# Hybrid mixer and experts layer on one core: keys projected first, zeros written by ScalarE, rotations placed ahead of the scores

## The reference

```python
h = rms_norm(x, norm_mix_g[i])
proj = h @ w_in[i]
y_s5 = s5_mixer(proj[..., :r0], ...)        # x[t] = lambda * x[t-1] + B u[t];  y = C x + D u
# RWKV-7: low-rank products of the shifted h
w_log = -softplus(-(w0 + tanh(xw @ w1) @ w2)) - 0.5
a = sigmoid(a0 + (xa @ a1) @ a2)
g = sigmoid(xg @ g1) @ g2
kk = heads(k * k_k);  kk = kk / max(norm(kk), 1e-12)
k = k * (1.0 + (a - 1.0) * k_a)
# per token: state = state * decay + (state . -kk) (kk * a)^T + v k^T;  y = state . r
```

## Time and profile before

| | value |
|---|---|
| median of 3 runs | 1267.28 us (1266.63 to 1267.98) |
| profiled execution | 1267.05 us |
| its span, first to last instruction | 1265.3 us |
| busy: VectorE, ScalarE, GpSimd | 402.3, 205.1, 28.3 us |
| read from memory | 427.89 MB, 339 GB/s over the span |
| mean granted TensorE clock | 0.972 of 2.4 GHz |

### The profile page before, as it was taken

How to read it: one execution, slowest core, us unless ns; L and a number is a source line. 1 busy time by engine, 2 the same in 40 slices (tenths; PEclk the granted TensorE clock), 3 DMA queues, 4 the chain that set the end, 5 groups by cost and what they waited for, 6 DMA issues and landing times. The chain is left out here.

```text
span 1265.3 us, 19269 instructions
## 1 busy us (share of the span) xinstructions
PE 1170.8 (93%) x8190; PEld 514.8 (41%) x8190; DVE 402.3 (32%) x750; ACT 205.1 (16%) x297; POOL 28.3 (2%) x16
## 2 busy tenths in 40 slices
PE   5889688958999999999999999999999999999997
PEld 4678586433333333333333333333333333333333
DVE  8928992572112122122112112211212112211222
ACT  2661012262000010011000001000011000000113
POOL 4100000020000000000000000000000000000000
PEclk8899888979999999999999999999999999999998
DMA  9300207235999999999999999999999999999960
GB/s 326 99 2 3 71 19 292 100 146 223 419 427 426 429 429 428 428 429 428 427 429 430 427 428 430 428 428 429 429 427 429 429 428 427 430 428 427 429 273 33
DMA packets 44237, 429.38 MB, mean 339 GB/s; under 512 B 4817, under 2 KB 15441, under 8 KB 19633
## 3 DMA queue, kind: packets, MB, share of 16 engines
q1 hardware_dynamic: 44016, 428.43, 80.9%
q0 software_dynamic: 192, 0.52, 0.1%
HBM read 427.89 MB, written 1.05 MB: 339 GB/s over the span
## 5 line engine op out<-in xcount | busy, mean ns | idle before, releaser
L1140 PE MATMUL bank<-arena 128*64 128x512 f32 (+5 forms) x5388 | 920.6, 479 | 24.7 <-DMA arena<-in_exp_w_up 19.1
L1140 PEld LDWEIGHTS bank<-arena 128*64 128x64 f32 (+4 forms) x5388 | 316.3, 128 | 605.3 <-issue 541.9
L221 PE MATMUL bank<-arena 64*64 64x64 f32 (+7 forms) x2032 | 175.0, 282 | 27.2 <-DVE arena L603 7.8
L221 PEld LDWEIGHTS bank<-arena 64*64 64x64 f32 (+3 forms) x2032 | 141.6, 160 | 59.8 <-issue 40.8
L1331 ACT ACTIVATE arena<-arena 128x512 f32<-128x512 f32 x32 | 20.1, 629 | 515.4 <-DVE arena L1375 515.4
L1390 DVE COPY arena<-bank 128x512 f32<-128x512 f32 x32 | 22.1, 691 | 234.9 <-PE bank L1140 234.9
L1380 DVE TENSOR_SCALAR arena<-bank 128x512 f32<-128x512 f32 x32 | 22.1, 691 | 211.8 <-PE bank L1140 211.8
L1375 DVE TENSOR_SCALAR arena<-bank 128x512 f32<-128x512 f32 x32 | 22.1, 691 | 188.8 <-PE bank L1140 188.8
L1334 ACT ACTIVATE arena<-bank 128x256 f32<-128x256 f32 x32 | 12.3, 383 | 310.1 <-PE bank L1430 310.1
L1351 DVE TENSOR_TENSOR arena<-bank,par 128x512 f32<-128x512 f32 x33 | 22.8, 692 | 76.4 <-PE bank L1140 76.4
L1331 ACT ACT_TABLE_LOAD x32 | 41.1, 1283 | 1.7 <-PEq L1162 1.2
(11 more groups left out here) (269 smaller groups left out, 459.8 us busy)
## 6 DMA issues: line engine op xcount, KB each, us to landing
arena<-in_exp_w_gate SPq DMA_DIRECT2D x64, 2048.0 KB, 23.4
arena<-in_exp_w_down SPq DMA_DIRECT2D x64, 2048.0 KB, 21.8
arena<-in_exp_w_up SPq DMA_DIRECT2D x64, 2048.0 KB, 25.3
arena<-in_w_in SPq DMA_DIRECT2D x8, 1024.0 KB, 12.1
arena<-in_w_out SPq DMA_DIRECT2D x4, 1024.0 KB, 5.5
arena<-in_ple_w_gate SPq DMA_DIRECT2D x2, 2048.0 KB, 21.7
arena<-in_xT SPq DMA_DIRECT2D x1, 1024.0 KB, 6.1
arena<-in_lora SPq DMA_DIRECT2D x1, 1024.0 KB, 13.6
```

The source lines that it names most:

```text
L221: return nc.tensor.matmul(out, lhsT, rhs, start=start, stop=stop, skip_group_check=True)
L1140: return nc.tensor.matmul(out, lhsT, rhs, start=start, stop=stop, skip_group_check=True)
```

## The change

- `order` becomes k, k, u, u, r, r, v, v. All counts on `proj_done` and `proj_copied` follow it, by `at_place`.
- The zeros are written by ScalarE (`clear`: a copy of one column of `par` with scale 0), in pieces, between its work of the start; those of `taps` come ahead of the tables. GpSimd writes none.
- The sum of squares uses `ones_early`, which VectorE fills, and waits for `eps_ready` instead of the constants' load. ScalarE's squares come behind the state-space exponentials and sines.
- The second low-rank product 1 goes to banks 2 and 3. Product 2 comes behind `project(2)`.
- TensorE: `project(3)`, the sums of the key norms, `project(4)` and `project(5)` come ahead of the taps; `into` follows `stack_u`.
- VectorE: the keys come ahead of the decays, output products and angles behind `k2`, and `phase_off(0)`, `phase_on(0)`, `phase_off(1)` together behind the receptance. `oprod` lies in other units.
- ScalarE's queue follows the others.

```diff
-oprod = [un(a).rearrange("p (n j c) -> p n j c", n=SUB, c=16) for a in (43, 25, 44)]
+oprod = [un(a).rearrange("p (n j c) -> p n j c", n=SUB, c=16) for a in (37, 25, 39)]
...
-root = un(24)[:, 0:T]
+root, ones_early = un(24)[:, 0:T], un(24)[:, 512:512 + P]
...
+LORA_BANK = (5, 2, 5)
...
-order = [0, 1, 4, 5, 2, 3, 6, 7]
+order = [4, 5, 0, 1, 2, 3, 6, 7]
+at_place = [order.index(q) + 1 for q in range(8)]
...
-    nc.gpsimd.memset(un(45), 0.0).then_inc(s["pads_clear"], 1)
-    nc.gpsimd.memset(un(16, 4), 0.0).then_inc(s["pads_clear"], 1)
-    nc.gpsimd.memset(un(20, 4), 0.0).then_inc(s["pads_clear"], 1)
...
-    pool.wait_ge(s["proj_done"], 2)
-    nc.gpsimd.memset(un(2, 2), 0.0).then_inc(s["pads_clear"], 1)
...
-    act.wait_ge(s["xT_in"], 16)
-    for b in range(2):
-        A(sq[:, 4 * b:4 * b + 4, :], xT[:, 4 * b:4 * b + 4, :], ACT.Square).then_inc(s["sq_ready"], 1)
+    def clear(a, n):
+        A(un(a, n), par[:, NPARAM:NPARAM + 1].to_broadcast([P, n * UNIT]), ACT.Copy, scale=0.0).then_inc(s["pads_clear"], 1)
+    act.wait_ge(s["eps_ready"], 1)
+    clear(45, 1)
+    clear(16, 2)
...
+    clear(18, 2)
...
+    act.wait_ge(s["xT_in"], 16)
+    for b in range(2):
+        A(sq[:, 4 * b:4 * b + 4, :], xT[:, 4 * b:4 * b + 4, :], ACT.Square).then_inc(s["sq_ready"], 1)
+    clear(20, 2)
+    clear(22, 2)
...
-    act.wait_ge(s["eps_ready"], 1)
...
-            src = banks[5 + i // 2][:, (i % 2) * T:(i % 2 + 1) * T]
+            src = banks[LORA_BANK[m] + i // 2][:, (i % 2) * T:(i % 2 + 1) * T]
...
-    act.wait_ge(s["pads_clear"], 2)
+    act.wait_ge(s["pads_clear"], 3)
...
-    act.wait_ge(s["pads_clear"], 3)
+    act.wait_ge(s["kk_ready"], 1)
+    A(kksq[:, :, :], kkn[:, :, :], ACT.Square).then_inc(s["kk_squared"], 1)
+    copy_proj(2)
+    lora_out(2)
+    act.wait_ge(s["decay_ready"], 1)
+    A(EL[:, :, :], Lc[:, :, :], ACT.Exp)
+    link(A(chunk_decay[:, :, :], Lc[:, :, CH - 1::CH], ACT.Exp))
+    A(Lc[:, :, :], Lc[:, :, :], ACT.Exp, scale=-1.0)
+    A(lw[:, :, :], lw[:, :, :], ACT.Exp).then_inc(s["exp_ready"], 1)
+    copy_proj(3)
+    act.wait_ge(s["kk_summed"], 1)
+    for b in range(2):
+        m = A(kb[:, 2 * b:2 * b + 2, :], banks[4 + b].rearrange("p (f t) -> p f t", t=T), ACT.Sqrt)
+    m.then_inc(s["kk_root"], 1)
+    act.wait_ge(s["pads_clear"], 5)
...
-    lora_out(2)
+    clear(2, 2)
...
-    copy_proj(2)
-    act.wait_ge(s["pads_clear"], 4)
+    copy_proj(4)
+    copy_proj(5)
+    act.wait_ge(s["pads_clear"], 6)
...
-    act.wait_ge(s["decay_ready"], 1)
...
-    copy_proj(3)
-    act.wait_ge(s["kk_ready"], 1)
-    A(kksq[:, :, :], kkn[:, :, :], ACT.Square).then_inc(s["kk_squared"], 1)
-    copy_proj(4)
-    act.wait_ge(s["kk_summed"], 1)
-    for b in range(2):
-        m = A(kb[:, 2 * b:2 * b + 2, :], banks[4 + b].rearrange("p (f t) -> p f t", t=T), ACT.Sqrt)
-    m.then_inc(s["kk_root"], 1)
-    for n in range(5, 8):
-        copy_proj(n)
+    copy_proj(6)
+    copy_proj(7)
...
+    V.memset(ones_early, 1.0)
...
-    dve.wait_ge(s["g_built"], 2)
-    products(oprod, "o_built", power[:, 0, 1:SUB + 1, :], power[:, 1, 1:SUB + 1, :], cc)
...
-    ts(un(46), un(46), PI, -PI, ALU.min, ALU.max).then_inc(s["table_arg"], 1)
...
+        if H:
+            dve.wait_ge(s["phase_on"], H)
...
-        dve.wait_ge(s["proj_done"], (4, 7)[H])
+        dve.wait_ge(s["proj_done"], (at_place[5], at_place[6])[H])
...
-    dve.wait_ge(s["proj_done"], 1)
-    link(V.memset(EL, 1.0))
-    link(V.memset(EL[:, :, 0::CH], 0.0))
-    dve.wait_ge(s["lora2_copied"], 2)
-    link(ts(lw, lw, -DECAY, None, ALU.mult))
-    link(V.tensor_tensor_scan(un(0), un(1), un(31), 0.0, ALU.mult, ALU.add))
-    tt(lw, Lc, lw, ALU.subtract).then_inc(s["decay_ready"], 1)
-    dve.wait_ge(s["proj_copied"], 4)
+    dve.wait_ge(s["proj_copied"], at_place[5])
...
+    dve.wait_ge(s["lora2_copied"], 2)
+    link(ts(lw, lw, -DECAY, None, ALU.mult))
+    dve.wait_ge(s["proj_done"], at_place[0])
+    link(V.memset(EL, 1.0))
+    link(V.memset(EL[:, :, 0::CH], 0.0))
+    link(V.tensor_tensor_scan(un(0), un(1), un(31), 0.0, ALU.mult, ALU.add))
+    tt(lw, Lc, lw, ALU.subtract).then_inc(s["decay_ready"], 1)
...
-    dve.wait_ge(s["o_padded"], 4)
-    V.memset(mag_run[:, :, 0:1], 0.0).then_inc(s["mag_ready"], 1)
-    phase_off(0)
+    products(oprod, "o_built", power[:, 0, 1:SUB + 1, :], power[:, 1, 1:SUB + 1, :], cc)
...
+    ts(un(46), un(46), PI, -PI, ALU.min, ALU.max).then_inc(s["table_arg"], 1)
...
-    dve.wait_ge(s["proj_done"], 5)
+    dve.wait_ge(s["proj_done"], at_place[2])
...
-    phase_on(0)
-    dve.wait_ge(s["proj_copied"], 6)
+    dve.wait_ge(s["o_padded"], 4)
+    V.memset(mag_run[:, :, 0:1], 0.0).then_inc(s["mag_ready"], 1)
+    dve.wait_ge(s["proj_copied"], at_place[3])
...
+    phase_off(0)
+    phase_on(0)
...
-    pe.wait_ge(s["consts_in"], 16)
+    pe.wait_ge(s["eps_ready"], 1)
...
-        last = mm(banks[7][:, 0:T], ones, sq[:, k, :], k == 0, k == KD - 1)
+        last = mm(banks[7][:, 0:T], ones_early, sq[:, k, :], k == 0, k == KD - 1)
...
+        pe.wait_ge(s["consts_in"], 16)
+        pe.wait_ge(s["lora2_copied"], 4)
...
-    for m in range(3):
+    def lora_second(m):
...
-            if m and i % 2 == 0:
-                pe.wait_ge(s["lora2_copied"], 2 * m - 2 + i // 2 + 1)
-            out = banks[5 + i // 2][:, (i % 2) * T:(i % 2 + 1) * T]
+            if m == 2 and i % 2 == 0:
+                pe.wait_ge(s["lora2_copied"], i // 2 + 1)
+            out = banks[LORA_BANK[m] + i // 2][:, (i % 2) * T:(i % 2 + 1) * T]
...
+    def head_sums(src, bank):
+        for b in range(2):
+            last = mm(banks[bank + b][:, :], head_ones, src[:, 2 * b:2 * b + 2, :], True, True)
+        return last
+    lora_second(0)
+    lora_second(1)
...
+    lora_second(2)
+    project(3)
+    pe.wait_ge(s["consts_in"], 16)
+    pe.wait_ge(s["kk_squared"], 1)
+    pe.wait_ge(s["lora2_copied"], 6)
+    head_sums(kksq, 4).then_inc(s["kk_summed"], 1)
+    project(4)
+    project(5)
...
-    project(3)
...
-    project(4)
-    pe.wait_ge(s["kk_squared"], 1)
-    pe.wait_ge(s["lora2_copied"], 6)
-    for b in range(2):
-        last = mm(banks[4 + b][:, :], head_ones, kksq[:, 2 * b:2 * b + 2, :], True, True)
-    last.then_inc(s["kk_summed"], 1)
-    project(5)
...
```

More of the change, by code:

```diff
@@ L376, in lora_out @@
                             last.then_inc(s["lora2_copied"], 1)
-                for n in range(2):
-                    copy_proj(n)
+                copy_proj(0)
+                copy_proj(1)
                 act.wait_ge(s["lora1_done"], 2)
@@ L572, in products @@
                     tt(b, wr, xi, ALU.mult).then_inc(s[built], 1)
-                    if built == "o_built":
-                        dve.wait_ge(s["g_padded"], 2)
                     link(tt(c, wi, xr, ALU.mult))
@@ L579, in _ @@
                 products(gprod, "g_built", coef[:, 0], coef[:, 1], bb)
-                dve.wait_ge(s["g_built"], 2)
-                products(oprod, "o_built", power[:, 0, 1:SUB + 1, :], power[:, 1, 1:SUB + 1, :], cc)
-                dve.wait_ge(s["consts_in"], 16)
-                dve.wait_ge(s["g_padded"], 4)
-                dve.wait_ge(s["o_built"], 2)
-                link(tt(tsin, con[:, C_TIME:C_TIME + NK][:, None, :].to_broadcast([P, NJ, NK]), th4[:, :, None].to_broadcast([P, NJ, NK]), ALU.mult))
-                reduce_angle(un(46), un(44), un(46))
-                ts(un(46), un(46), PI, -PI, ALU.min, ALU.max).then_inc(s["table_arg"], 1)
                 def phase_off(H):
@@ L657, in _ @@
                 link(tt(k2, k2, kx, ALU.mult))
-                dve.wait_ge(s["o_padded"], 4)
-                V.memset(mag_run[:, :, 0:1], 0.0).then_inc(s["mag_ready"], 1)
-                phase_off(0)
+                products(oprod, "o_built", power[:, 0, 1:SUB + 1, :], power[:, 1, 1:SUB + 1, :], cc)
+                dve.wait_ge(s["consts_in"], 16)
+                dve.wait_ge(s["g_padded"], 4)
+                link(tt(tsin, con[:, C_TIME:C_TIME + NK][:, None, :].to_broadcast([P, NJ, NK]), th4[:, :, None].to_broadcast([P, NJ, NK]), ALU.mult))
+                reduce_angle(un(46), un(44), un(46))
+                ts(un(46), un(46), PI, -PI, ALU.min, ALU.max).then_inc(s["table_arg"], 1)
                 dve.wait_ge(s["kk_root"], 1)
@@ L842, in stack_u @@
                 def stack_u():
-                    pe.wait_ge(s["proj_copied"], 2)
+                    pe.wait_ge(s["proj_copied"], at_place[1])
                     for b in range(2):
@@ L945, in _ @@
                 pe.wait_ge(s["scores_copied"], 6)
-                for b in range(2):
-                    last = mm(banks[b][:, :], head_ones, rk[:, 2 * b:2 * b + 2, :], True, True)
-                last.then_inc(s["rk_summed"], 1)
+                head_sums(rk, 0).then_inc(s["rk_summed"], 1)
                 for lev in range(LEVELS):
```

## The result

The changed kernel takes 1248.47 us, the median of four runs (1247.59 to 1249.34), against 1267.63 for the kernel before in the same set. The ratio is 0.985, with a 95% interval of 0.9833 to 0.9867. The forecast was 1249.9, in a range of 1247 to 1256. The difference of 19.2 us between these medians is far outside the spread of either kernel. The profiled execution took 1249.34 with a span of 1247.5, 17.7 us less than the profiled one of before.

A forecast was written before the change was run, and what follows sets the result against it. TensorE was taken as the bound of the mixer, except VectorE at 127 to 135 us. Gains 0.9 + 6.6 + 0.7 + 8.8 + 0.2 = 17.2 us off 1267.05 gave 1249.9 us, range 1247 to 1256.

The forecast's parts named there:

- The start: Before the first projection: zeros moved to ScalarE let the squares and the root's reciprocal come earlier; gain 0.9 us.
- rival 2: First projection: TensorE's clock stays up after a shorter pause, about 2 us more gained until `xa` limits, 1248 us; chance 0.08.
- Low-rank products and the third projection: TensorE, 49.66 to 66.87 us: without waiting for ScalarE's copies, 17.21 us becomes 10.6; gain 6.6 us.
- Taps, turns and stacking: TensorE after the receptance: lengths kept, into(0) waits 0.7 us for the last `ustack` copy, 8.18 becomes 7.5; gain 0.7 us.
- The cover at the taps: ScalarE must finish pads, zeros, tables and two copies before TensorE ends the taps at about 86.1 us; 0.7 us left.
- Rival 1: ScalarE comes late to the taps: TensorE waits 2.7 us, half clock costs up to 1.9 more, 1254 us; chance 0.18.
- Scores: First mask earlier by 8.8 us beyond earlier gains as the wait for the rotation goes, plus 0.2 in the mask row.
- the list of signs: Expected trace signs, among them TensorE's wait for ScalarE at turn_g's start staying near zero and first mask near 118.
- Rivals 3: Start: VectorE's first operation keeps its 8.70 us, caused by GpSimd's own start; 5.1 us lost, 1256 us; chance 0.04.
- 4: After the mixer: gain moved and not kept, expert stream starts by something unseen; 1267 us; chance 0.04.
- 5: Middle: ScalarE becomes the bound, reaching the taps copies so late that the gain is eaten; 1270 at 20 us late; chance 0.03.

The follow-up runs named there:

- run 1: Changed kernel with all zeros written by GpSimd again, ScalarE's queue otherwise as changed; 1251.74 us, first level mask at 134.47 us instead of 129.99.
- run 2: Changed kernel with zeros on GpSimd and ScalarE squaring x ahead of everything else, as before the change; 1251.15 us, first level mask at 132.59 us.
- run 12: The changed kernel itself, unedited, timed once more on the chip of the later runs; 1249.22 us, first level mask at 129.56 us.
- run 3: Changed kernel with second low-rank products in banks 5 and 6 only and product 2 ahead of project(2), as before; 1256.07 us.
- run 8: Changed kernel with the whole value projection project(6) moved between the taps and the turns; first level mask at 131.00 us instead of 129.99.
- run 9: Changed kernel with only the first half of project(6) between taps and turns; 1244.95 us, ratio to the kernel before 0.9823.
- run 10: Changed kernel with phase_on(1) moved from behind the bonus to right behind phase_off(1); 1246.84 us, ratio to the kernel before 0.9836.
- run 7: Changed kernel with ScalarE writing the zeros of the taps four times instead of once, ahead of the tables; 1252.22 us.
- run 5: Changed kernel with phase_off(0) back ahead of the norm of the keys and phase_on(0) behind the scaled arrays; 1264.84 us.
- run 6: Kernel before the change with only the rotations moved behind the receptance; 1269.6 us against 1266.4 for the kernel before beside it.
- run 4: Changed kernel with state-space input projected before the keys, VectorE and ScalarE queues reordered to fit, key-norm sums behind project(4); 1250.44 us.
- run 11: Changed kernel with 14 extra matmuls of ones on TensorE between the sum of squares and the first projection; 1250.59 us.

## Why the prediction was right

- **The start, forecast 0.9, measured 1.7.** The mechanism is shown by runs 1 and 2. The size was off in ScalarE's queue: the two first zeros took 2.85 us instead of 3.15 and those of 2048 columns 1.91 instead of 2.1, so the squares began at 8.97 and not at 9.8.
- **The clock of the first projection (rival 2), forecast 2 us if it stays up.** It was at 0.51 in the profiled execution and at 1.00 in run 12, and between these two it made no difference; where it stayed at 0.50 for longer, in runs 3, 8, 9 and 10, it cost about 0.5 us. The rival's limit, `xa` at 39.5, should have been `xw`: the low-rank products wait for it at 35.3 to 35.7 us, so the gain ends there.
- **Low-rank products and the third projection, forecast 6.6, measured 7.8** (47.67 to 66.87 before, 46.00 to 57.42 now), the largest error in a term. Product 2 took 1.7 us from start to start, near the 1.9 that I had. Product 1 is the mis-sized piece: I gave it 1.9 us as well, but behind product 0 it added 0.9. Each of them alone took 2.0 us before, both together take 2.9 (46.00 to 48.89); they use 64 rows each, and from 46.97 their matmuls start 0.11 us apart instead of 0.22. Run 3, which undoes this part, costs 7.7 in its own stretch.
- **Taps, turns and stacking, forecast 0.7, measured 0.0.** From the taps' start to the last projection's end it was 58.4 us, and it is 58.4 from the corresponding point. The new wait for the stacked copy is the 0.7 us that I had (L439). Project(3) with a pause of 0.9 us inside took 8.0 us before; without it and with the new wait it is 7.6, so 0.4 were won there and not 0.7. The rest is in differences of 0.1 to 0.2 us between parts that I took as equal.
- **The cover at the taps, forecast 0.7 us of room, measured 1.4.** Run 7 shows how little that is: with 5.8 us more on ScalarE, TensorE stood 3.85 us longer. Rival 1 was the near danger, as stated, and did not occur; its own sum, 2.7 + 1.9, is 4.6 and not 4.2, which leaves its 1254 within half a microsecond. Loads of tables ran without a drain: the next root began at 67.12 behind a load of 1.28 us from 65.83.
- **Scores, forecast 8.8 + 0.2, measured 8.5 + 0.4.** 125.23 - 115.82 = 9.4 us were won up to the last projection, 17.9 at the first mask, 18.25 at the first level mask. The last rotation ended at 112.93, forecast 113.6. Runs 5 and 6 show that the place of the rotations and the place of `into` are one decision: either without the other loses.
- **Two readings of the rows that were wrong.** VectorE did not run without a pause behind its 22.8 us: it waited 5.2 us for the root of the key norms (L663), which is the wait that run 6 makes longer. And TensorE's wait for ScalarE at the turns could not stay near zero, as the list of signs had it: it was 2.1 us before and is 2.1 us now. Neither entered the sum, since the stretch of the turns was carried over with its pause inside.
- **Sum, forecast 17.2, measured 18.25 at the mark**, 17.7 between the profiled executions and 19.2 between the medians; the rest of the kernel moves by up to 3 us from run to run. The terms were off by 0.8, 1.2, -0.7, -0.3 and 0.2 us: the mechanisms are the ones forecast, but that the sum is off by only 1.0 is in part that these errors cancel. Rivals 3, 4 and 5 did not occur: VectorE's first operation took 0.17 us, and nothing was taken back behind the mixer.

## What to carry to other kernels

When two engines take turns in waiting for each other, look for work of the bound engine that can stand where the other's answer is due; which data comes first matters less than that (run 4), and a consumer must move with its producer (runs 5 and 6). Price a pause of TensorE with the half clock that may follow it: at the turns it cost from nothing to 1.6 us, with the same instructions. Follow the queue of the engine that takes over cheap work, here ScalarE's zeros: it had 1.9 us of room, and the change lived inside it. Half a projection in a gap was worth more than a whole one (runs 8 and 9).

## What the runs showed that I had not expected

The same program with the same pause of 3.03 us ahead of its first projection had TensorE's clock at 0.51 in one execution and at 1.00 in another (19 to 22 us). Over all runs with a pause of 3.0 to 3.1 us there, the clock stayed at 1.00 in runs 1, 5, 7 and 12 and fell in the first profile and in runs 3, 8, 9 and 10. Behind the pause of 2.1 us at L567 it was 1.00 in runs 1, 5, 7 and 12 and 0.79 in run 11, and behind the one at the turns it fell in six of eleven executions. Whether the clock falls behind a pause of 2 to 3 us was not settled by the length of the pause here, and keeping TensorE busy with empty work in one place did not protect the next. For whoever reads single traces this means that a difference of a microsecond has to be placed first: an edit is priced in its own stretch, and what comes in another is looked at by itself.
